# Prompt attention with scores kept keys by queries: a first pass for the maxima, division at the end

## The chip, the cores and the metric

The kernel runs on one core of one Trainium2 chip. The metric is the time of one execution on the device in microseconds (us). TensorE is called PE in the profile (PEld is its weight load), VectorE DVE, ScalarE ACT, GpSimd POOL, SyncE SP.

## The reference

A two-layer encoder for 1024 prompt tokens and 32 sample tokens, width 1024. In each layer an input projection feeds three groups of attention heads, whose outputs are normalised, projected and followed by a convolutional feed-forward block. What changes is the attention of the prompt in two groups: the forget-gate heads (FoX, six of 64 columns) and the latent heads (MLA, four with 96 columns of keys and 64 of values).

```python
s = jnp.einsum('bqhd,bkhd->bhqk', qb, k) * scale
if fk is not None:                     # FoX only: running sums of log forget gates
    s = s + F_query - F_key
s = jnp.where(allowed, s, NEG_INF)     # FoX: key <= query; MLA: by chunks of 64
p = jax.nn.softmax(s, axis=-1)
return jnp.einsum('bhqk,bkhd->bqhd', p, v)
```

## The kernel before

Stages follow one another in blocks with semaphores of their own. `mixers` (L2417) calls for each layer: FoX prompt attention, FoX sample attention, windowed (SWA) prompt and sample attention, preparation of MLA, MLA prompt and sample attention, and a norm. The three prompt stages are one function, `attend_prompt` (L921).

Heads go in pairs (three for FoX, two for MLA), and a pair in eight rounds of 128 queries. A round turns the pair's queries and keys with transposes on PE (L1040, L1041, 128 x 64 or 128 x 96), ACT copies their high part as float32r and DVE subtracts to get the low part (L1115, L1116, L1161, L1164). Scores are queries x keys: stationary queries of 128, moving keys of up to 512, three products (high x high, high x low, low x high, L1068), and on the diagonal an identity matmul that adds the mask (L1072). DVE takes the row maxima, negated (L1186); ACT takes the exponential with that as its bias and its sum beside it (L1144); DVE takes the reciprocal of the sum (L1192), and DVE or POOL multiplies the probabilities by it (L1198, L1029). PE turns each 128 x 128 of them (L1092), ACT and DVE copy them to SBUF (L1131, L1207, L1209), and PE multiplies them with the values, both heads of the pair into the two halves of one bank (L1105, 64 stationary columns, float32, so two records for a matmul in the trace). ACT copies the result to yT (L1152).

The order is written by hand: each engine walks a list of units (a round of both heads up to four key tiles, then one head a unit), turns tiles three rounds ahead, and PE does the scores of unit m, the transposes of unit m-2 and the values of unit m-3. The rows of the forget gates, high and low part, come by DMA into the operand of the keys (L1011). POOL and DVE clear what the operands pad (L1022, L1168).

Of the kernel before, what the change touches and what calls it, by code (L numbers as in the profile page):

```python
# [203 lines left out]
class Load:  # L204
# [67 lines left out]
    def scalar_first(self, act):  # L272
        k = self.k
        act.wait_ge(self.const_in, 16)
        act.activation(k.identr[:, :], k.const[:, C_ID:C_ID + P], ACT.Copy)
        act.activation(k.mfoxr[:, :], k.const[:, C_MFOX:C_MFOX + P], ACT.Copy)
        act.activation(k.mmlar[:, :], k.const[:, C_MMLA:C_MMLA + P], ACT.Copy)
        act.wait_ge(self.vec_turned, 1)
        for l in range(DEPTH):
            last = act.activation(k.vec[l][:, :], self.bank[:, 7, 2 * l * P:2 * l * P + V_N], ACT.Copy)  # L280
        last.then_inc(self.vec_ready, 1)
# [593 lines left out]
def fox_rows(nc, k, prep, frow):  # L875

    with ExitStack() as s:  # L880
        ps = s.enter_context(nc.psum_tensor("fps" + k.tag, [P, 2, 512], F32))
        psF = s.enter_context(nc.psum_tensor("fpsF" + k.tag, [P, QT, P], F32))
        sem = k.sems["fox"]
        f_done, copied, f_turned, row_hi = (sem[n] for n in ("f", "fc", "ft", "rh"))
        tri, ones = k.const[:, C_TRI:C_TRI + P], k.const[:, C_ONE:C_ONE + P]
        lf, cl, pre, fp, fs = prep.g[:, 5], prep.cl, prep.pre, prep.fp, prep.fs
        with nc.Block() as block:

            @block.sync
            def _(sp):  # L890
                sp.wait_ge(prep.stored, 16 * prep.STORES)

            @block.tensor
            def _(pe):
                pe.matmul(ps[:, 0, 0:QT * FOXH], tri, lf[:, 0:QT, :], start=True, stop=False)
                pe.matmul(ps[:, 0, 0:QT * FOXH], ones, pre[:, 0, 0:QT, :], start=False, stop=True)
                pe.matmul(ps[:, 1, 0:TT * FOXH], tri, cl[:, :, :], start=True, stop=False)
                pe.matmul(ps[:, 1, 0:TT * FOXH], ones, pre[:, 1], start=False, stop=True).then_inc(f_done, 1)
                pe.wait_ge(copied, 1)
                for t in range(QT):  # L900
                    last = pe.transpose(psF[0:FOXH, t, :], fp[:, t, :], k.const[:, C_ID:C_ID + P])
                last.then_inc(f_turned, 1)

            @block.scalar
            def _(act):
                act.wait_ge(f_turned, 1)
                act.activation(frow[0][:, :], psF[0:FOXH, :, :].rearrange("p t n -> p (t n)"), ACT.Copy,
                               scale=-1.0).then_inc(row_hi, 1)

            @block.vector  # L910
            def _(dve):
                dve.wait_ge(f_done, 1)
                dve.tensor_copy(fp[:, :, :], ps[:, 0, 0:QT * FOXH].rearrange("p (t h) -> p t h", h=FOXH))\
                   .then_inc(copied, 1)
                dve.tensor_copy(fs[:, :, :], ps[:, 1, 0:TT * FOXH].rearrange("p (t h) -> p t h", h=FOXH))
                dve.wait_ge(row_hi, 1)
                dve.scalar_tensor_tensor(frow[1][:, :], psF[0:FOXH, :, :].rearrange("p t n -> p (t n)"), -1.0,
                                         frow[0][:, :].bitcast(F32), ALU.mult, ALU.subtract)


def attend_prompt(nc, k, kind, heads, kdim, q_of, k_of, v_of, kv_of, yT, yc, frow=None, alibi=None):  # L921
# [739 lines left out]
class ProjectOut:  # L1661
# [18 lines left out]
    def cols(self, o):  # L1680
        return slice((o % NT) * TN, (o % NT + 1) * TN)
# [678 lines left out]
@contextmanager  # L2360
def own_semaphores(nc, name, singles, several=()):

    with ExitStack() as s:
        one = lambda n: s.enter_context(nc.semaphore(f"{name}_{n}"))
        sem = {n: one(n) for n in singles.split()}
        for n, m in several:
            sem[n] = [one(f"{n}{i}") for i in range(m)]
        yield sem
        restart(nc, [x for v in sem.values() for x in (v if isinstance(v, list) else [v])])
# [47 lines left out]
def mixers(nc, k, lay, places, proj, prep, used):  # L2417
# [11 lines left out]
    with ExitStack() as f:  # L2429
        keep(f, "small_kept", places.LOW - places.SMALL)  # L2430
        fs = prep.fs
        with ExitStack() as f2:
            frow = [f2.enter_context(nc.sbuf_tensor("frow" + n + k.tag, [FOXH, SEQ], F32R)) for n in ("hi", "lo")]
            fox_rows(nc, k, prep, frow)
            cols = lambda o: (lambda h: proj[:, :, o + HD * h:o + HD * (h + 1)])
            attend_prompt(nc, k, "fox", FOXH, HD, cols(O_FQ), cols(O_FK),
                          lambda h, t: proj[:, t, O_FV + HD * h:O_FV + HD * (h + 1)], lambda h: h, yT, 0, frow=frow)
        kc = f.enter_context(nc.sbuf_tensor("fkc" + k.tag, [P, QT, FOXH * HD], F32))
        vc = f.enter_context(nc.sbuf_tensor("fvc" + k.tag, [P, QT, FOXH * HD], F32))
        loads = [(dst[:, a:b, :], src[lay, 0].rearrange("(t p) h d -> p t (h d)", p=P)[:, a:b])  # L2440
                 for dst, src, a, b in ((kc, k.cache_fox_k, 0, 4), (kc, k.cache_fox_k, 4, QT), (vc, k.cache_fox_v, 0, QT))]
        tiles = [(P, lambda u, t=t: kc[:, t, P * u:P * (u + 1)], lambda p, t=t: vc[:, t, P * p:P * (p + 1)])
                 for t in range(QT)]
        tiles.append((DEC, lambda u: proj[0:DEC, QT, O_FK + P * u:O_FK + P * (u + 1)],
                      lambda p: proj[0:DEC, QT, O_FV + P * p:O_FV + P * (p + 1)]))
        attend_sample(nc, k, "fox", FOXH, lambda u: proj[0:DEC, QT, O_FQ + P * u:O_FQ + P * (u + 1)], FOXH // 2, P,
                      lambda h: HD * (h % 2), tiles, loads, yT, 0, fs, SwaHeads(nc, k, lay, f, proj))
# [15 lines left out]
    with ExitStack() as f:  # L2463
        qm = rt("qm", [P, TT, MLAH, MQK], where=f)
        km = rt("km", [P, 2 * QT + 1, MLAH, MQK], where=f)
        vm = rt("vm", [P, 2 * QT + 1, MLAH, HD], where=f)
        mla_prepare(nc, k, lay, proj, qm, km, vm)
        left.close()
        attend_prompt(nc, k, "mla", MLAH, MQK, lambda h: qm[:, :, h, :], lambda h: km[:, :, h, :],
                      lambda h, t: vm[:, t, h, :], lambda h: h, yT, 6)  # L2470
        tiles = [(P if j < QT else DEC, lambda u, j=j: km[0:P if j < QT else DEC, QT + j, u, :],
                  lambda p, j=j: vm[0:P if j < QT else DEC, QT + j, 2 * p:2 * p + 2, :].rearrange("p h d -> p (h d)"))
                 for j in range(TT)]
        attend_sample(nc, k, "mla", MLAH, lambda h: qm[0:DEC, QT, h, :], MLAH, MQK, lambda h: HD * (h % 2), tiles,
                      [], yT, 6)
# [52 lines left out]
```

## Time and profile before

| | us |
|---|---|
| median of 3 runs | 3335.85 |
| lowest and highest | 3334.83, 3339.76 |
| the profiled execution | 3335.93 |
| its span | 3333.8 |
| busy PE, DVE, ACT, POOL | 2998.4, 1566.6, 991.1, 863.2 |
| granted clock of TensorE, mean | 0.934 |

A name in a group is a tile with its stage (psSfox are the scores of the FoX stage). Shapes are partitions x elements. Matmuls are pipelined: the duration of one contains its modelled end, so their price is read from the distances between starts. "Idle before" is the time in which the engine had nothing, with what ended it.

### The profile page before, as it was taken

To read this page: it belongs to the slowest core of one execution; us is meant where nothing else is said; L and a number is where in the kernel's file an instruction comes from. 1 tells how busy PE (TensorE), PEld (TensorE's weight loads), DVE (VectorE), ACT (ScalarE), POOL (GpSimd) and SP (SyncE) were. 2 spreads that over 40 slices of the span, in tenths; PEclk is the share of its full clock that TensorE was granted. 3 is DMA by queue.
4 is the path that set the end of the run, shared out by engine and by line. 5 is a ranking of instruction groups with operands and counts; after the bars stand their busy time and mean duration, and the time that the engine had idled before them with its cause. 6 is when DMAs were issued, how large, how long until landed. Compare 5 with 4: busy or idle time off the path is not lost. (4 is left out here: it accounts for less than half of the span.)

```text
span 3333.8 us, 50479 instructions
## 1 busy us (share of the span) xinstructions
PE 2998.4 (90%) x19996; PEld 2804.0 (84%) x19996; DVE 1566.6 (47%) x2734; ACT 991.1 (30%) x2175; POOL 863.2 (26%) x489
## 2 busy tenths in 40 slices
PE   5998977686999999999999988876679999999998
PEld 5997745465999999999899975645579999999998
DVE  3326646743244444444442465657343444444443
ACT  3224525544321111111242254454333111111111
POOL 3111142103332322222341122311044222222230
PEclk8998958787999999999999988787889999999999
DMA  5110010001511111111122101000024111111111
GB/s 174 44 41 23 2 48 18 1 1 56 177 51 51 38 50 50 38 50 38 55 89 59 40 3 40 10 17 1 14 92 153 45 44 50 38 50 38 50 50 53
DMA packets 181249, 161.81 MB, mean 49 GB/s; under 512 B 17236, under 2 KB 168316, under 8 KB 180860
## 3 DMA queue, kind: packets, MB, share of 16 engines
q1 hardware_dynamic: 181116, 160.02, 15.4%
q8 instruction: 85, 1.39, 0.2%
q14 instruction: 48, 0.39, 0.0%
HBM read 129.97 MB, written 30.13 MB: 48 GB/s over the span
## 5 line engine op out<-in xcount | busy, mean ns | idle before, releaser
L1942 PE MATMUL bank_b<-x_hi,fwhi 128*128 128x352 f32 x2112 | 690.5, 327 | 5.3 <-POOL fwlo L1898 5.3
L1942 PE MATMUL bank_b<-x_hi,fwlo 128*128 128x352 f32 x2112 | 688.9, 326 | 0.0
L1942 PE MATMUL bank_b<-x_lo,fwhi 128*128 128x352 f32 x2112 | 687.3, 325 | 0.0
L1898 POOL TENSOR_TENSOR fwlo<-raw,fwhi 128x1024 fp32r<-128x1024 f32 x132 | 322.2, 2441 | 583.5 <-ACT fwhi L2023 569.8
L1942 PEld LDWEIGHTS bank_b<-x_hi,fwhi 128*128 128x128 f32 x2112 | 400.0, 189 | 6.5 <-POOL fwlo L1898 5.9
L1942 PEld LDWEIGHTS bank_b<-x_lo,fwhi 128*128 128x128 f32 x2112 | 402.2, 190 | 0.0
L1942 PEld LDWEIGHTS bank_b<-x_hi,fwlo 128*128 128x128 f32 x2112 | 398.6, 189 | 0.6
L2131 DVE TENSOR_TENSOR fx<-fx,bank_b 128x352 f32<-128x352 f32 x528 | 275.6, 522 | 233.3 <-PE bank_b L1972 233.3
L1972 PE MATMUL bank_b<-fuhi,fwhi 128*128 128x352 f32 x1056 | 344.5, 326 | 10.3 <-DVE fx L2131 5.7
L1972 PE MATMUL bank_b<-fulo,fwhi 128*128 128x352 f32 x1056 | 344.8, 326 | 0.0
L1972 PE MATMUL bank_b<-fuhi,fwlo 128*128 128x352 f32 x1056 | 344.2, 326 | 0.0
L2043 ACT ACTIVATE fuhi<-fcb 128x1024 fp32r<-128x1024 f32 x44 | 46.7, 1061 | 696.3 <-PE bank_b L1972 550.7
L1907 POOL TENSOR_TENSOR fcb<-fcb,rsb 128x1024 f32<-128x1024 f32 x44 | 96.8, 2201 | 510.9 <-ACT fcb L2037 510.9
L1972 PEld LDWEIGHTS bank_b<-fuhi,fwhi 128*128 128x128 f32 x1056 | 201.5, 191 | 14.1 <-DVE fx L2131 9.1
L543 PE MATMUL bank_a<-whi,x_hi 128*128 128x246 f32 (+1 forms) x648 | 183.4, 283 | 17.7 <-POOL x_lo L320 10.9
L1972 PEld LDWEIGHTS bank_b<-fulo,fwhi 128*128 128x128 f32 x1056 | 199.1, 189 | 0.0
L1972 PEld LDWEIGHTS bank_b<-fuhi,fwlo 128*128 128x128 f32 x1056 | 198.8, 188 | 0.0
L543 PE MATMUL bank_a<-whi,x_lo 128*128 128x246 f32 (+1 forms) x648 | 183.1, 283 | 0.0
L543 PE MATMUL bank_a<-wlo,x_hi 128*128 128x246 f32 (+1 forms) x648 | 183.1, 283 | 0.0
L543 PE MATMUL bank_b<-whi,x_lo 128*128 128x246 f32 (+1 forms) x648 | 180.8, 279 | 0.0
L543 PE MATMUL bank_b<-wlo,x_hi 128*128 128x246 f32 (+1 forms) x648 | 180.7, 279 | 0.0
L543 PE MATMUL bank_b<-whi,x_hi 128*128 128x246 f32 (+1 forms) x648 | 179.8, 278 | 0.0
(409 smaller groups left out, 5968.4 us busy)
## 6 DMA issues: line engine op xcount, KB each, us to landing
raw<-in_w_ffn_up SPq DMA_DIRECT2D x88, 512.0 KB, 3.8
raw<-in_w_ffn_down SPq DMA_DIRECT2D x44, 512.0 KB, 3.6
wraw<-in_w_in SPq DMA_DIRECT2D x18, 984.0 KB, 5.5
xs<-x_between SPq DMA_DIRECT2D x16, 528.0 KB, 3.9
x_between<-xs SPq DMA_DIRECT2D x16, 528.0 KB, 2.6
fx<-x_between SPq DMA_DIRECT2D x2, 4224.0 KB, 13.2
raw<-in_w_out SPq DMA_DIRECT2D x16, 512.0 KB, 5.2
x_between<-fx SPq DMA_DIRECT2D x3, 1408.0 KB, 6.3
```

The costliest lines, as they stand in the source:

```text
L543: last = pe.matmul(bank[0:n, t % NB, 0:WN], a[:, c, at], w[b][:, c, :], start=(c == 0 and m == 0), stop=(c == DC - 1 and m == 2))
L1898: pool.tensor_tensor(self.wlo[:, r], self.raw[:, o % 2], self.whi[:, r].bitcast(F32), ALU.subtract)\
L1907: pool.tensor_tensor(v, v, self.rsb[:, 0:SEQ], ALU.mult)
L1942: last = pe.matmul(bank[:, first_bank + t, 0:TN], w[:, role, c, :], x[:, c, self.cols(t)], start=(c == 0 and m == 0), stop=(c == DC - 1 an ...
L1972: last = pe.matmul(bank[:, 6 + o % 2, 0:TN], w[:, D0 + e, m, :], x[:, e, self.cols(t)], start=(e == 0 and i == 0), stop=(e == 1 and i == 2))
L2043: act.activation(uhi[:, e, 0:SEQ], cb[:, e, 0:SEQ], ACT.Copy)
L2131: dve.tensor_tensor(x, x, bank[:, 6 + o % 2, 0:TN], ALU.add).then_inc(self.p_out[o % 2], 1)
```

## The change

FoX and MLA prompt attention call a new function, `attend_keys`; SWA keeps `attend_prompt`. The new function goes by pair of heads and half of the queries (u, 512 queries), and in it by key tile (b, 4 or 8 of 128). Scores stand keys x queries, so that their exponentials are what the value matmul needs, without a transpose. The maximum of each query must be known before: a first pass multiplies only the high parts, queries x keys, and DVE reduces it (masked tiles by an add of a mask table and a minimum in one operation). The maxima are turned by PE, split in high and low parts and laid as extra rows into the query operand, against rows of ones in the keys, so that the score matmul subtracts them. Exponentials are summed over key tiles on POOL (first head) and DVE (second head), a matmul with ones adds them over partitions, and each half's output is multiplied by the reciprocal (512 columns, both heads) at the end. First-pass units of the next half, and the turning of later tiles, are hosted in the steps of the current one. The masks of the score matmul are made at launch, turned over. Here `bank_free(pe, item)` waits until the item two before it in the two banks psT has been read (for denominators: `inverted`).

```diff
+    XS = 2
+    NP = 3
+    nb = lambda u: HT * (u % 2 + 1)
+    first_col = lambda u, b: max(b - HT * (u % 2), 0) * P
+    def max_units(u):
+        if u % 2 == 0:
+            return [(e, j, 0, (j + 1) * P, True) for j in range(HT) for e in range(2)]
+        return [(e, j, a, w, a > 0) for j in range(HT) for a, w in ((0, HALF), (HALF, (j + 1) * P)) for e in range(2)]
+    def hosted_tiles(u, b):
+        p = u // 2
+        if u % 2 == 0:
+            return [(p, HT + 2 * b), (p, HT + 2 * b + 1)] if b < 2 else []
+        return [(p + 1, b)] if b < HT and p + 1 < pairs else []
+    def hosted_units(u, b):
...
+        if u % 2 == 0:
+            at = (0, 4, 10, 16, 16)
+        else:
+            at = (0, 0, 0, 0, 2, 4, 6, 8, 8)
+        return units[at[b]:at[b + 1]]
...
+        def sum_up(eng, u, b, e, done):
...
+                eng.tensor_tensor(acc[:, e, c:HALF], acc[:, e, c:HALF], new, ALU.add).then_inc(done, 1)
...
+            def _(pool):
+                for n, (rows, value) in enumerate(((mc[:, :, :, :, :], 1.0), (qh[R0:K2].bitcast(F32), 1.0),
+                                                   (kh[R0:K2].bitcast(F32), 1.0), (mtab[:, 0:HALF - P], 0.0))):
+                    pool.memset(rows, value).then_inc(cleared, 1)
+                    pool.wait_ge(cleared, n + 1)
...
+                def first_pass(u, units):
...
+                        if n >= 2:
+                            pe.wait_ge(maxed, n - 1)
...
+                        pe.matmul(psS[:, n % 2, 0:w], qh[0:K1, s, e, j * P:(j + 1) * P], kh[0:K1, p % 2, e, a:a + w],
+                                  start=True, stop=True).then_inc(scored, 1)
...
+                def maxima(u):
+                    pe.wait_ge(maxed, unit_base[u + 1])
...
+                            last = pe.transpose(psT[0:NA, bank_of[item] % 2, j * P:(j + 1) * P], mc[:, u % 2, j, e, :],
+                                                ident)
...
+                def scores(u, b):
...
+                        pe.matmul(out[:, c:HALF], kh[0:K2, p % 2, e, keys], qh[0:K2, s, e, c:HALF], start=True, stop=False)
+                        pe.matmul(out[:, c:HALF], kl[0:kdim, p % 2, e, keys], qh[0:kdim, s, e, c:HALF], start=False,
+                                  stop=False)
+                        last = pe.matmul(out[:, c:HALF], kh[0:K2, p % 2, e, keys], ql[0:K2, s, e, c:HALF], start=False,
+                                         stop=not diag)
...
+                def values(u, b):
+                    p, n, c = u // 2, step_no[(u, b)], first_col(u, b)
+                    pe.wait_ge(expd, 2 * n + 2)
+                    if b == 0 and u:
+                        pe.wait_ge(y_done, u)
...
+                def denominators(u):
...
+                        last = pe.matmul(psT[HD * e:HD * e + HD, bank_of[item] % 2, :], ones, acc[:, e, :],
+                                         start=True, stop=True)
...
+                pe.wait_ge(cleared, 3)
+                for i in range(HT):
+                    turn(0, i)
+                first_pass(0, max_units(0))
+                maxima(0)
+                for u, b in steps:
+                    for p, i in hosted_tiles(u, b):
+                        turn(p, i)
+                    scores(u, b)
+                    if b == 0 and u:
+                        denominators(u - 1)
+                    first_pass(u + 1, hosted_units(u, b))
+                    if b:
+                        values(u, b - 1)
+                    if b == nb(u) - 1:
+                        if u + 1 < NU:
+                            maxima(u + 1)
+                        values(u, b)
+                denominators(NU - 1)
...
+                        if diag:
...
+                            dve.tensor_tensor_reduce(ps, ps, mtab[:, HALF - w:HALF], -1.0, m if a else -BIG, ALU.add,
+                                                     ALU.min, m).then_inc(maxed, 1)
+                        else:
+                            dve.tensor_reduce(m, ps, AX, ALU.max, negate=True).then_inc(maxed, 1)
...
+                def divide(u):
+                    p, s = divmod(u, 2)
+                    dve.wait_ge(den_done, u + 1)
+                    dve.reciprocal(rec[:, :], psT[:, bank_of[("den", u)] % 2, :]).then_inc(inverted, 1)
+                    dve.wait_ge(inverted, u + 1)
+                    dve.wait_ge(mixed, step_no[(u, nb(u) - 1)] + 1)
+                    dve.tensor_tensor(yT[:, yc + p, s * HALF:(s + 1) * HALF], psO[:, :], rec[:, :], ALU.mult)\
+                       .then_inc(y_done, 1)
...
+                for u, b in steps:
+                    for p, i in hosted_tiles(u, b):
+                        low_part(p, i)
+                    if b == 0 and u:
+                        divide(u - 1)
+                    first_pass(u + 1, hosted_units(u, b))
+                    if b >= 2:
+                        sum_up(dve, u, b - 1, 1, sum1)
+                    if b == nb(u) - 1:
+                        if u + 1 < NU:
+                            maxima(u + 1)
+                        sum_up(dve, u, b, 1, sum1)
```

In `mixers` the two calls are replaced; FoX hands over tiles of 128 columns (a pair in one transpose), MLA one head at a time.

## Rows read from the trace of the kernel before

**Rows 1.** Page, part 1: busy time of each engine over the span

```profile
PE 2998.4 (90%) x19996; PEld 2804.0 (84%) x19996; DVE 1566.6 (47%) x2734; ACT 991.1 (30%) x2175; POOL 863.2 (26%) x489
```

**Rows 2.** Windows: stretch, length, busy of PE, PEld, DVE, ACT, POOL, granted clock

```profile
285.30:414.00 128.70, 117.86 (x1008) 100.99 (x1008) 86.28 (x182) 73.30 (x204) 22.31 (x17) 0.93 0.01 2
631.90:721.00 89.10, 80.73 (x672) 69.48 (x672) 55.96 (x120) 49.01 (x136) 10.02 (x8) 0.91 0.00 1
285.30:298.00 12.70, 8.05 (x35) 6.81 (x36) 6.12 (x12) 3.44 (x13) 7.89 (x6) 0.50 0.02 3
```

**Rows 3.** Timeline (start us, us, engine): first value matmuls of two head pairs

```profile
302.75 0.33 PE L1105 MATMUL psOfox<-pTfox,proj 128*64 128x128 f32 x2
340.73 0.33 PE L1105 MATMUL psOfox<-pTfox,proj 128*64 128x128 f32 x2
```

**Rows 4.** Timeline: starts of neighbouring score matmuls, 512, 384, 256 and 128 columns

```profile
1995.27 0.40 PE L1068 MATMUL psSfox<-kThifox,qTlofox 96*128 96x512 f32 x1
1995.51 0.34 PE L1068 MATMUL psSfox<-kThifox,qThifox 96*128 96x384 f32 x1
1995.68 0.34 PE L1068 MATMUL psSfox<-kTlofox,qThifox 96*128 96x384 f32 x1
...
332.20 0.28 PE L1068 MATMUL psSfox<-kTlofox,qThifox 96*128 96x256 f32 x1
332.32 0.28 PE L1068 MATMUL psSfox<-kThifox,qTlofox 96*128 96x256 f32 x1
...
2003.51 0.27 PE L1068 MATMUL psSfox<-kThifox,qTlofox 96*128 96x128 f32 x1
2003.62 0.27 PE L1072 MATMUL psSfox<-mfoxr,identr 128*128 128x128 f32 x1
```

**Rows 5.** Timeline: eight transposes; 32 records of value matmuls, what follows them

```profile
345.44 1.06 PE L1092 MATMUL psTfox<-const,prfox 128*128 128x128 f32 x8
...
336.19 1.97 PE L1105 MATMUL psOfox<-pTfox,proj 128*64 128x128 f32 x32
338.09 0.50 PE L1068 MATMUL psSfox<-kThifox,qThifox 96*128 96x512 f32 x1
338.43 0.40 PE L1068 MATMUL psSfox<-kTlofox,qThifox 96*128 96x512 f32 x1
```

**Rows 6.** Groups by form: operation, shapes, count, busy us, mean ns

```profile
L1186 DVE TENSOR_REDUCE stfox<-psSfox 128x2 f32<-128x512 f32 x3 | 2.1, 691 | 4.1 <-PE psSfox L1072 4.1
L1161 DVE TENSOR_TENSOR qTlofox<-psXfox,qThifox 64x256 fp32r<-64x256 f32 x24 | 9.8, 408 | 4.9 <-ACT kThifox L1116 4.8
L1144 ACT ACTIVATE prfox<-psSfox,stfox 128x512 f32<-128x512 f32 x6 | 4.1, 682 | 0.0
...
L1182 DVE TENSOR_TENSOR psSswa<-psSswa,biasswa 128x512 f32<-128x512 f32 x42 | 29.1, 693 | 6.3 <-PE psSswa L1068 5.4
```

**Rows 7.** Groups by form, one line (min/median/max ns): reciprocals, six-column add

```profile
L1192 DVE RECIPROCAL stfox<-stfox 128x2 f32<-128x2 f32 x12 | 1.8, 153 | 0.0
...
L665 DVE RECIPROCAL rs<-rs 128x8 f32<-128x8 f32 x1 | 0.2, 205 | 4.8 <-ACT rs L657 4.8
...
L823 DVE TENSOR_TENSOR fpre<-fpre,fcl x16: 156/158/167, 257.2 to 1897.7; 128x6 f32<-128x6 f32 x16
```

**Rows 8.** Timeline: GpSimd and VectorE, both with two SBUF inputs

```profile
998.12 2.58 POOL L1898 TENSOR_TENSOR fwlo<-raw,fwhi 128x1024 fp32r<-128x1024 f32 x1 [24.00 <-ACT fwhi L2023]
998.36 2.38 DVE L2125 TENSOR_TENSOR fulo<-fcb,fuhi 128x32 fp32r<-128x32 f32 x1
```

**Rows 9.** Timeline: a memset and the first score of the forget-gate stage

```profile
285.31 1.80 POOL L1022 MEMSET kThifox<- 32x2048 f32 x1 [50.04 <-POOLq L887]
...
292.76 0.46 PE L1068 MATMUL psSfox<-kThifox,qThifox 96*128 96x128 f32 x1
```

**Rows 10.** Timeline: last write of that stage; transposes after an idle TensorE, second layer

```profile
412.96 0.28 ACT L1152 ACTIVATE yT<-psOfox 128x128 f32<-128x128 f32 x1 [2.20 <-PE psOfox L1105]
...
2043.41 1.39 PE L1092 MATMUL psTfox<-const,prfox 128*128 128x128 f32 x8 [1.96 <-DVE pTfox L1209]
```

More of the change, by code:

```diff
@@ L275, in scalar_first @@
         act.activation(k.identr[:, :], k.const[:, C_ID:C_ID + P], ACT.Copy)
-        act.activation(k.mfoxr[:, :], k.const[:, C_MFOX:C_MFOX + P], ACT.Copy)
-        act.activation(k.mmlar[:, :], k.const[:, C_MMLA:C_MMLA + P], ACT.Copy)
+        one = k.const[:, C_ONE:C_ONE + P]
+        act.activation(k.mfoxr[:, :], k.const[:, C_TRI:C_TRI + P], ACT.Copy, scale=-BIG, bias=BIG)
+        act.activation(k.mmlar[0:CHUNK, :], one[0:CHUNK], ACT.Copy, scale=0.0)
+        act.activation(k.mmlar[CHUNK:P, 0:CHUNK], one[CHUNK:P, 0:CHUNK], ACT.Copy, scale=BIG)
+        act.activation(k.mmlar[CHUNK:P, CHUNK:P], one[CHUNK:P, CHUNK:P], ACT.Copy, scale=0.0)
         act.wait_ge(self.vec_turned, 1)
@@ L2435, in mixers @@
             cols = lambda o: (lambda h: proj[:, :, o + HD * h:o + HD * (h + 1)])
-            attend_prompt(nc, k, "fox", FOXH, HD, cols(O_FQ), cols(O_FK),
-                          lambda h, t: proj[:, t, O_FV + HD * h:O_FV + HD * (h + 1)], lambda h: h, yT, 0, frow=frow)
+            attend_keys(nc, k, "fox", FOXH, HD,
+                        lambda p, i: [(proj[:, i, o + P * p:o + P * (p + 1)], P, w, 0) for w, o in ((0, O_FQ), (1, O_FK))],
+                        lambda h, t: proj[:, t, O_FV + HD * h:O_FV + HD * (h + 1)], yT, 0,
+                        k.const[:, C_MFOX:C_MFOX + P], k.mfoxr[:, :], frow)
         kc = f.enter_context(nc.sbuf_tensor("fkc" + k.tag, [P, QT, FOXH * HD], F32))
@@ L2468, in mixers @@
         left.close()
-        attend_prompt(nc, k, "mla", MLAH, MQK, lambda h: qm[:, :, h, :], lambda h: km[:, :, h, :],
-                      lambda h, t: vm[:, t, h, :], lambda h: h, yT, 6)
+        attend_keys(nc, k, "mla", MLAH, MQK,
+                    lambda p, i: [(x[:, i, 2 * p + e, :], MQK, w, e) for w, x in ((0, qm), (1, km)) for e in range(2)],
+                    lambda h, t: vm[:, t, h, :], yT, 6, k.const[:, C_MMLA:C_MMLA + P], k.mmlar[:, :])
         tiles = [(P if j < QT else DEC, lambda u, j=j: km[0:P if j < QT else DEC, QT + j, u, :],
```

199 lines of the change are left out of this document (added).

## The prediction

> **What bounds the kernel now.** I read the page first: TensorE (PE) is busy for 90% of the span [rows 1], so the first question of every stage is how much work its PE stream holds. Then the windows of the stages that change: forget-gate (FoX) attention lasts 128.7 us in the first layer, latent (MLA) attention 89.1 us, and in both PE is busy for over 90% while VectorE (DVE) has 86 and 56 us of work [rows 2]. The second layer repeats them, so some 435 us of 3334 are at stake. Then the timeline. One pair of heads takes 340.73 - 302.75 = 38.0 us [rows 3]. Next to that I set the PE stream of one pair, by distances between starts: a score matmul costs 0.24 us at 512 columns, 0.17 at 384, 0.12 at 256, 0.11 at 128 [rows 4]. One pass over one head's causal tiles is 0.64 us for each set of 512, 384, 256, 128 and there are two such sets and four more of 512, so 2.24 us. Three passes and eight masks of 0.09 make 7.4 us a head, 14.9 a pair. A transpose costs 0.11 us (eight in 1.06, of which the last 0.27 is modelled end), so 72 of probabilities cost 7.9 and 32 of queries and keys 3.5. A 128-column value matmul is two records of 0.055 us, and 72 cost 7.9. A change to or from the 64-column value matmuls costs about 0.3 us: after 32 records the next score starts 1.90 us later instead of 1.76, and the one behind it after 0.34 instead of 0.24 [rows 5]; eight such breaks are 2.4. The sum, 36.6 us, is nearly the 38.0 measured. The stage is bound by the PE stream. Around three pairs lie a front, 7.5 us to the first score [rows 9] at half clock [rows 2], and a short tail.
>
> **PE stream after the change.** Scores are the same area turned over, again 14.9 us a pair. The first pass adds one pass for each head, +4.5. The 72 transposes go, -7.9. FoX turns two heads in one transpose, -1.8 (MLA: nothing). Value matmuls cover the same area, 7.9; they are now 12 visits instead of 8, and two for denominators come on top, so breaks go from 2.4 to 4.2. Denominators: two matmuls of 512 columns for each half, at 4 x 0.11 each, +1.8. Turning the maxima: 16 transposes, +1.8. Together 14.9+4.5+1.8+7.9+4.2+1.8+1.8 = 36.9 us against 36.6. What the transposes give, the new operations take; PE's stream gains nothing. So the answer lies in who waits.
>
> The Trainium skill, TensorEngine Tiling (Array Packing), section Key Properties, says that changing the tiling mode drains TensorE; the 0.3 us above is how this trace shows it, and by that rule each of the six extra visits a pair costs the same whatever its width.
>
> **DVE after the change.** For a pair: low parts of eight tiles, four of 128 columns each (the 256-column one takes 0.41 [rows 6]; I take 0.25 at 128), 8.0 us for FoX, 6.0 for MLA. Reductions of the first pass: eight plain ones of 512 at 0.69 [rows 6] = 5.5, and 16 masked ones. The masked one is an operation that this trace lacks. Its nearest row is the add of 512 columns into PSUM, 0.69 [rows 6]; I take that, with 0.29, 0.42, 0.56 for the shorter ones: 4 x 1.96 = 7.8. The upper bound is twice that, as if it were an add and a reduction. Running sums of the second head: 5.5. Low parts of the maxima: four of 512 columns, 2.8. Last the division, once for each half: a reciprocal of 512 columns, then a multiply of 0.69. No such reciprocal is in the trace. Eight columns take 0.205 us, two take 0.153, while a six-column add takes 0.158 [rows 7]: 0.052/6 = 8.6 ns a column, eight times an ordinary one. So 512 columns take 0.15 + 512 x 0.0083 = 4.4 us. Bounds: 0.69 (as an ordinary operation) and 4.6. I take 4.4, since the slope is read from rows of this very operation. Two divisions make 10.2 us a pair. DVE's sum is 39.8 us a pair, 120 for FoX instead of 86: more than PE's 111.
>
> The Trainium skill, VectorE: DVE Perf Modes, "First, the fixed hardware budget", says that the reciprocal is an iterated divide with a repeat count of 8. By that rule 512 columns take 8 x 512 cycles; the rows above agree in slope.
>
> **Where these waits fall.** DVE and PE run in order, and the first pass has two PSUM buffers, so PE stops at the third unit of a batch until DVE has reduced the first.
>
> Half of queries 0-511 (even), which hosts the 16 units of the next half. PE holds 14 us of work, DVE 16.4 and the division 5.1. The chain: PE turns two tiles, scores, denominators, to 3.4; division to 8.6; four reductions to 10.4; PE, stopped until then, turns two tiles, ACT and DVE split them to 14.0; six reductions to 17.9; PE values and scores to 19.2; six reductions and a sum to 24.2; the last maxima are turned, copied (0.6), split (0.7) for two heads, to 27.9. Before the next half's scores nothing can go. So 28 us, 22.5 without a division for the first.
>
> Half of queries 512-1023 (odd). PE holds 22.3 us. The second score of step 1 takes the bank of the denominators, so it waits for the reciprocal: 4.4 less 0.9 of work, 3.5 lost. The maxima at its end lose 1.3 behind the last values. So 27 us, 23 in the last pair, which hosts nothing.
>
> Front: PE first waits for three memsets on GpSimd, the largest of 4096 columns. 2048 take 1.80 us [rows 9], so 0.2+1.8+3.6 = 5.6 us in which it used to turn tiles. Four tiles through two buffers, ACT and DVE to 13.1, eight first-pass reductions to 17.0, the maxima to 20.7. FoX 20.7 instead of 7.5, MLA about 17 instead of 6.
>
> Tail: denominators, reciprocal, multiply after the last value matmul: 1.4+4.4+0.8 = 6.6.
>
> FoX: 20.7+22.5+27+28+27+28+23+6.6 = 182.8 instead of 412.96+0.28-285.3 = 127.9 [rows 10]: +55. MLA: 17+21.5+27+27+23+6.6 = 122.1 instead of 88: +34. Both layers: +178.
>
> Granted clock: PE stood for 2.0 us in the second layer and the eight transposes behind it took 1.39 instead of 1.06 [rows 10], [rows 5]; the front runs at 0.50, the 1.2 GHz level [rows 2]. The new stage lets PE stand for 3.5 to 5 us at each division. I take 1 us lost at each of the 16 inner ones, with bounds 0 and 3: +16.
>
> ACT loses the accumulator reads and the copies of turned probabilities; a 512-column exponential is 0.68 us or less [rows 6], 35 us in a FoX stage, beside 26 of splits, under PE. GpSimd sums the first head beside it. The four extra constants at launch lie under loads: 0, at most 1 us. SyncE's row transfers wait for the second memset group and land before the first unit in my front.
>
> Sum against the profiled execution (3335.9 us with what lies around the span, the median of the runs within 0.1 us): 3336+178+16 = **3530 us**.
>
> **Rivals.** (a) The reciprocal streams at one column a cycle, 0.7 us. An even half then loses 3.7 us, an odd one 3.5, the tail 3.7, and the clock stays: 20 divisions x 3.6 = 72, and 16 less, 3442 us. Against it: the slope in [rows 7]. (b) GpSimd and DVE block each other. A 32-column subtraction with two SBUF inputs took 2.38 us and ended with GpSimd's operation begun before it [rows 8]. The new running sums run on both engines with two SBUF inputs. Each DVE sum could wait up to 1 us; 9 a pair, of which a third falls where DVE is the bound: 3 x 10 pairs = +30, and with it the masked reduction at double price, +3.9 for each even half: +39. 3600 us. For it: the row; against: in the odd halves DVE has slack.
> The Trainium skill, GPSIMD Engine Reference, section Key points, says the two engines share SBUF interfaces; by this rule the wait of (b) is due on each overlapping sum, and the row on blocking agrees.
> (c) Faster: the long value matmuls hide the mode change. Then the 14 breaks cost nothing, -4.2 a pair, and if the reciprocal also costs under 1 us, DVE (30 us a pair) is hidden in PE's 32.7: FoX 98+15 (front beyond the work already counted)+3 = 116, -12; MLA -8; 3296 us. It decides from a reciprocal under 1 us and a break under 0.1. (d) The change works as meant but only balances, PE bound with reciprocal cheap and breaks as now: FoX 111+15+3 = 129, within 0.2%: 3336.
>
> **How the numbers follow.** Forecast 0.62, (a) 0.14, (b) and more lost clock 0.14, (c) 0.06, (d) 0.04. The range leaves out (c), (d) and the outer part of (b): 3420 (rival (a) less 20 for my waits being too long) to 3600. Faster by over 0.2% (what a measurement of this kernel can tell) 0.06, within 0.2% 0.04, slower 0.90.
>
> **What would show it.** The reciprocal's row near 4.4 us, twenty of them; PE idle released by it for about 3.5 us in odd halves; first-pass matmuls waiting for DVE's reductions in even ones; the first full score some 20 us into the stage; the FoX window near 185 us and MLA near 125. A reciprocal row of 0.7 us, or DVE sums of 1 us and more, would prove the term wrong.

## The result: 389 us slower, twice the forecast

| | before | after |
|---|---|---|
| median, us | 3337.4 | 3726.2 |
| lowest and highest | 3334.8, 3339.8 | 3695.1, 3739.1 |
| span of the profiled execution | 3333.8 | 3731.8 |
| granted clock of TensorE, mean | 0.934 | 0.863 |

The ratio is 1.1155, with a 95% interval of 1.1122 to 1.1187. The forecast was 3530 us, its range ended at 3600: the direction was right, the time outside. +389 us came where +194 were forecast.

The profile page of the kernel after, part 1, stands against [rows 1]; its two lines for PE and the clock in 40 slices follow.

```profile
PE 3300.8 (88%) x18700; PEld 2812.8 (75%) x18700; DVE 1669.5 (45%) x2976; ACT 959.9 (26%) x2033; POOL 919.9 (25%) x569
...
PE   6997996757599999999999899885767999999999
...
PEclk9995556867799999999999855577768999999999
```

PE counts 302 us more of busy time with fewer instructions, while its stream was forecast to be no longer. The clock line says where: in slices 4 to 6 and 24 to 26, the FoX stages, TensorE was granted half its speed. The windows of the kernel after (stretch, length, busy of PE, PEld, DVE, ACT, POOL, granted clock) answer to [rows 2]: the FoX stage, three of its halves of queries (an odd one, queries 512 to 1023; an even one, 0 to 511; the last, odd as well, which hosts no first pass), the MLA stage.

```profile
281.00:562.60 281.60, 244.00 (x601) 112.82 (x600) 116.91 (x274) 69.53 (x181) 35.47 (x38) 0.54 0.00 1
345.50:395.50 50.00, 47.08 (x117) 21.23 (x117) 18.46 (x47) 13.18 (x33) 7.28 (x7) 0.57 0.00 1
395.50:431.70 36.20, 31.80 (x83) 15.59 (x83) 19.82 (x44) 9.64 (x27) 2.56 (x5) 0.55 0.00 1
520.10:561.90 41.80, 38.35 (x83) 15.64 (x83) 8.09 (x9) 6.48 (x13) 6.74 (x7) 0.53 0.00 0
783.60:916.40 132.80, 105.08 (x432) 60.91 (x432) 72.62 (x150) 38.18 (x88) 24.16 (x25) 0.78 0.00 1
```

DVE has 117 us of work in 282: it isn't the bound it was forecast to be. PE is busy 244 us at a clock of 0.54, where the stage before had 0.93.

So I went to the spacing of the score matmuls, the view of [rows 4]. Timeline of the kernel after, PE and its weight loads (start, duration, line, in brackets the idle time before): a FoX score at full clock, then one at half clock.

```profile
337.96 0.50 PE L1119 MATMUL psTfox<-qhifox,khifox 67*128 67x512 f32 x1 [0.38 <-DVE qlofox L1227]
338.39 0.18 PEld L1120 LDWEIGHTS psTfox<-qhifox,klofox 64*128 64x128 f32 x1 [0.24 <-issue]
338.39 0.50 PE L1120 MATMUL psTfox<-qhifox,klofox 64*128 64x512 f32 x1
338.82 0.19 PEld L1122 LDWEIGHTS psTfox<-qlofox,khifox 67*128 67x128 f32 x1 [0.25 <-issue]
...
342.35 0.78 PE L1119 MATMUL psTfox<-qhifox,khifox 67*128 67x512 f32 x1
343.06 0.79 PE L1120 MATMUL psTfox<-qhifox,klofox 64*128 64x512 f32 x1
343.78 0.79 PE L1122 MATMUL psTfox<-qlofox,khifox 67*128 67x512 f32 x1
```

Matmuls of 512 columns start 0.43 us apart at full clock, against 0.24 in [rows 4], and 0.71 us apart at half. The weight load waits for "issue", no engine. The operands tell why: 67, then 64, then 67 contraction rows. A head's 64 columns, two rows for the forget gate and one for the maximum make 67; the low part of the keys has no such rows, and the code takes `kl[0:kdim]`, 64. The kernel before padded all to 96. MLA has 97, 96 and 97 rows, and its spacing is not widened (0.24 us at full clock). So the theory A of the experiments: a product of 64 rows between products of 67 drains TensorE twice (I call a drain the gap that such a change leaves), and a drained TensorE is then kept slow.

To see where each run's time lies I give the stages from the timelines: FoX from the first gate matmul to the end of the last write of yT (the gate work before the stage, about 5 us, is in all of them), MLA from the last write of the windowed heads to its own last one. Each of the other stretches agrees within 5 us in all runs.

| run | median, us | FoX, layers 1 and 2 | MLA, layers 1 and 2 |
|---|---|---|---|
| before | 3337 | 132.9, 132.9 | 172.4, 172.8 |
| after | 3726 | 284.8, 279.9 | 219.7, 222.8 |
| e1_pad | 3629 | 221.8, 222.8 | 221.2, 220.3 |
| e2_copy | 3642 | 253.3, 248.6 | 206.3, 206.1 |
| e3_before64 | 3398 | 163.6, 163.5 | 173.1, 172.4 |
| e4_pad_copy | 3541 | 184.4, 203.9 | 206.1, 205.2 |
| e5_three | 3573 | 216.1, 217.5 | 205.5, 205.4 |
| e6_nofirst | 3477 | 190.1, 172.3 | 187.3, 188.2 |
| e7_all | 3588 | 215.5, 224.9 | 207.4, 210.0 |
| e9_nofirst_raw | 3507 | 230.6, 225.7 | 172.8, 175.4 |
| e10_fill | 3566 | 203.7, 215.7 | 207.1, 203.6 |
| e11_fill_raw | 3729 | 296.3, 300.0 | 204.1, 209.4 |
| e12_before_fill | 3331 | 130.9, 130.0 | 171.0, 170.6 |

After against before: +152 and +147 in FoX (forecast 55 and the clock), +47 and +50 in MLA (forecast 34 and the clock).

### The profile page after: what moved, and what is told of

Its sections match the earlier page's. It is cut to its first block and busy times, and to the rows that moved or that the text cites. A ratio compares the mean times of both kernels' runs of the same rounds, so it can differ in the third digit from the quotient of the medians.

```text
span 3731.8 us, 48237 instructions
## 1 busy us (share of the span) xinstructions
PE 3300.8 (88%) x18700; PEld 2812.8 (75%) x18700; DVE 1669.5 (45%) x2976; ACT 959.9 (26%) x2033; POOL 919.9 (25%) x569
```

## Experiments: the drains, the divisions, and both

**e1_pad**

```diff
+                pool.memset(kl[R0:K2].bitcast(F32), 0.0).then_inc(cleared, 1)
...
-                        pe.matmul(out[:, c:HALF], kl[0:kdim, p % 2, e, keys], qh[0:kdim, s, e, c:HALF], start=False,
+                        pe.matmul(out[:, c:HALF], kl[0:K2, p % 2, e, keys], qh[0:K2, s, e, c:HALF], start=False,
```

> The change with the three rows 64 to 66 of the low keys cleared and the second FoX score product made with 67 contraction rows instead of 64, so that all products of a FoX score have the same rows; the output stays the same. Theory A (a product of 64 rows between products of 67 drains TensorE twice, and the drained engine is then held at the 1.2 GHz level): the 512-column spacing in a FoX score goes from 0.43 us (full clock) and 0.71 us (half clock) to 0.24 and 0.43, the granted clock of the FoX stage rises from 0.50-0.59 to the 0.8 of MLA, the FoX stage goes from some 281 us to about 190, near the 183 of the prediction, and the time falls by about 170 us to some 3555. Rival B (the clock is low because TensorE stands at divisions and behind the reductions of the first pass; the drains are only their own 0.2 to 0.3 us): 72 scores a stage, two changes each, give 30 us a stage, the clock stays under 0.6, and the time is about 3665. Rival C (contraction rows don't matter): 3726.

Measured 3629.2 us (3612.7 to 3634.1), ratio to before 1.0883 (1.0864 to 1.0902): -97 us by the medians, all of it in FoX (-63 and -57 in the profiled executions, of which that of e1_pad was its fastest). That lies between A (3555) and B (3665), nearer to B. The windows of the padded run: an odd, an even and the last half of FoX.

```profile
338.10:370.10 32.00, 28.77 (x117) 15.36 (x117) 19.58 (x48) 12.96 (x33) 6.23 (x7) 0.77 0.01 1
370.10:402.00 31.90, 25.98 (x83) 14.70 (x83) 19.84 (x46) 9.50 (x27) 3.63 (x5) 0.60 0.00 1
464.20:498.60 34.40, 30.91 (x83) 15.71 (x83) 8.12 (x10) 6.48 (x13) 6.15 (x7) 0.55 0.00 0
```

The odd half fell from 50.0 to 32.0 us, its clock rose from 0.57 to 0.77. The even half hardly moved and stayed at 0.60. So the drains are one cause, and there is a second that lowers the clock.

**e2_copy** and **e4_pad_copy**

```diff
-                    dve.reciprocal(rec[:, :], psT[:, bank_of[("den", u)] % 2, :]).then_inc(inverted, 1)
+                    dve.tensor_copy(rec[:, :], psT[:, bank_of[("den", u)] % 2, :]).then_inc(inverted, 1)
```

> The change with a plain copy of 512 columns in the place of each of the 20 reciprocals; it leaves out the division, so its output is not the reference's. Theory A (the low clock comes from the drains): each division gives back up to 3.36 - 0.69 = 2.7 us, 53 us in all if every one lies on the path, fewer in the FoX stages, whose clock stays under 0.6: 3675 to 3700. Rival B (TensorE standing at the divisions keeps the clock down): the clock of FoX returns to over 0.8 and the time falls by 150 us or more, to below 3580.

> Both edits at once: rows padded to 67 and a copy instead of the reciprocal (leaves out the division, so its output is not the reference's). It shows what the change costs beside these two. Theory A: some 3555 less 53 to 70 us (each division 2.7, or more where the clock is lost behind it): 3490 to 3500, the FoX clock over 0.85, and what is left over the 3336 of the kernel before lies in the fronts (13 us each) and in the halves bound by VectorE. Rival B: the same time as with the copy alone, less 60.

Measured 3642.4 us (3612.0 to 3655.0; 1.0901, 1.084 to 1.0962) and 3540.8 (3528.2 to 3543.8; 1.0616, 1.0598 to 1.0634). Both lie between the theories, 3675 for A and 3580 for B in the first, 3500 and 3582 in the second. Without the reciprocal 84 us go from the drained kernel and 88 from the padded one: 4.2 and 4.4 us a division, where 3.36 - 0.69 = 2.7 is all that DVE saves. The rest I put down to the clock, and the windows say how. First e2_copy: two odd halves of FoX in one execution, 120 and 119 matmuls, and the last half. Then e4_pad_copy: an odd half, and the last half in the first and in the second layer.

```profile
343.10:394.20 51.10, 51.10 (x120) 22.78 (x119) 15.89 (x48) 14.75 (x38) 7.41 (x7) 0.50 0.00 1
426.70:456.50 29.80, 29.09 (x119) 13.84 (x118) 16.64 (x48) 14.41 (x37) 7.29 (x7) 1.00 0.00 1
490.30:530.50 40.20, 39.47 (x86) 16.11 (x85) 5.50 (x10) 7.08 (x14) 7.22 (x7) 0.50 0.00 0
```

```profile
393.00:417.10 24.10, 23.05 (x119) 13.17 (x117) 16.77 (x48) 13.96 (x37) 7.43 (x7) 1.00 0.00 1
446.20:464.10 17.90, 17.11 (x84) 9.05 (x83) 8.00 (x10) 7.08 (x14) 7.26 (x7) 1.00 0.00 0
2180.60:2212.90 32.30, 31.52 (x85) 15.97 (x84) 5.44 (x10) 7.08 (x14) 7.24 (x7) 0.50 0.00 1
```

The same work took 29.8 or 51.1 us, and 17.9 or 32.3 us, by the level of the clock with which it was entered, and kept that level from its start to its end. The second pair has no change of rows: a padded stream too can stay at half clock for a whole half, with PE busy for 31.5 of 32.3 us.

The two kernels differ in the rows alone, so halves at one level of the clock price a change of rows: 29.8 - 24.1 = 5.7 us for the 32 changes of an odd half at full clock, 0.18 us each, and 40.2 - 32.3 = 7.9 us for the 32 of the last half at half clock, 0.25 us each. For the 288 changes of both layers that makes 51 and 71 us, an estimate from these halves. So more than half of the 97 us of e1_pad is the changes' own price; the rest I put down to the clock, which rose in the odd halves.

The two levels are also the likeliest reason for the spread of the kernel after (44 us where the kernel before has 5); that I have only argued.

**e3_before64**

```diff
+                                    rows = slice(0, HD if fox and x else None)
-                                    last = pe.matmul(bank[:, 0:n], qT[x][:, r % RQ, e, :],
-                                                     kT[y][:, p % 2, e, f + a:f + a + n],
+                                    last = pe.matmul(bank[:, 0:n], qT[x][rows, r % RQ, e, :],
+                                                     kT[y][rows, p % 2, e, f + a:f + a + n],
```

> The kernel before, with the last of its three FoX score products made with 64 contraction rows instead of 96 (the 32 rows left out are zeros, the output stays the same). It adds only the change of rows, twice in each of the 72 scores of a stage, to a stage without division at the end and without a first pass. Theory A: each change costs 0.2 us, 29 us a stage at full clock, and the granted clock of the stage falls from 0.93 as well; together between 3395 (clock kept) and 3520 (clock at half), I expect 3480. Rival B: 3395 and the clock above 0.85. Rival C: 3336.

Measured 3397.8 us (3395.2 to 3399.3), ratio 1.0186 (1.0169 to 1.0203): +60.5 us, rival B's number to 3 us. The mean granted clock of the span is 0.930 (before 0.934). The windows of this run say what part is clock: the beginning of the FoX stage, and 40 us in its middle.

```profile
299.00:313.80 14.80, 14.80 (x54) 9.45 (x53) 6.26 (x15) 6.07 (x19) 4.40 (x3) 0.50 0.01 1
...
340.00:380.00 40.00, 39.91 (x291) 27.96 (x291) 24.01 (x55) 21.88 (x62) 5.01 (x4) 1.00 0.01 1
```

At full clock a pair of heads takes 398.06 - 352.33 = 45.7 us between its last writes of yT, where the kernel before has 376.19 - 338.21 = 38.0: 7.75 us for 24 scores with two changes each, 0.16 us a change, 46 us in six pairs. The other 14 us are the clock: it came back at 313.8 us, in the kernel before at 299.9, though PE did not stand in between. Once back it stayed for 119 us. The Trainium skill, TensorEngine Tiling (Array Packing), sections Tiling Modes and Key Properties, has a mode for up to 64 contraction rows beside that for 128 and says that a change of mode drains TensorE; this run agrees.

## Experiments: what lowers the clock

**e6_nofirst** and **e9_nofirst_raw**

```diff
     def hosted_units(u, b):
-        if u + 1 == NU:
-            return []
+        return []
```

> The change with padded rows, and without the first pass of all halves but the first: its matmuls and reductions are left out, with the exponential taken at a scale of 0.001 so that it stays finite (its output is not the reference's). The divisions, the turning of the maxima and all else stay. Theory D: the clock of the even halves goes from 0.5-0.6 to above 0.9, an even half from 32-34 us to about 17 (11 of TensorE's work, 3.5 at the division, 3 at the maxima) and an odd one from 28-32 to 25 to 28: about 3440. Rival E (the stand of 3 to 4 us at each division lowers the clock by itself): the even halves lose only the 6 us of work and stops of the first pass, the clock stays under 0.7: about 3570.

> The change with 64 rows left as they are (not padded), without the first pass of all halves but the first, and with a copy instead of the reciprocal (leaves out both, exponentials at a scale of 0.001; its output is not the reference's). The drains stay, and hardly any stop is left. Theory F (drains don't lower the clock, they only keep a lowered one from coming back): the FoX clock is above 0.9, odd halves take 29 to 30 us, even ones about 17, and the time is about 3440. Rival A (the drains alone pull the clock down): the FoX clock stays under 0.65, odd halves take 50 us, and the time is about 3590.

Measured 3476.6 us (3459.7 to 3500.2; 1.0437, 1.0382 to 1.0493) and 3507.1 (3482.1 to 3527.7; 1.0489, 1.0435 to 1.0544), in the middle of the rivals both (3440 and 3570, 3440 and 3590). The diff shows the edit that they share; e6 has the padded rows beside it, e9 the copy. Without the first pass the padded kernel gives back 153 us. MLA's even half fell from 31.5 to 14.2 us at a clock of 1.00 (theory D; 18.2 at 0.72 in the second layer), a part of it the work left out, but the FoX halves behind a division are still slow, at 0.50 to 0.72, and the last one has its 34.4 us again (theory E). Both kinds of stop lower the clock: DVE's hold on the first pass and the division.

Behind its front e9 has neither, and drains alone. The windows of e9_nofirst_raw: an odd half of FoX, the last half of FoX, and an odd half of MLA.

```profile
402.80:451.30 48.50, 48.50 (x115) 21.03 (x114) 12.36 (x31) 14.93 (x39) 7.60 (x7) 0.50 0.00 1
468.50:508.70 40.20, 39.40 (x85) 16.03 (x85) 5.45 (x10) 7.10 (x14) 7.22 (x7) 0.50 0.00 0
764.00:787.20 23.20, 23.03 (x127) 13.61 (x125) 11.94 (x23) 12.59 (x29) 8.13 (x7) 1.00 0.00 1
```

Here PE is counted busy for all 48.5 us and stays at the 1.2 GHz level: I had expected 30 us and 1.00 (theory F). And the drained stream did not only fail to come back, it also fell. Three windows of its second layer, one behind the other:

```profile
2131.00:2179.10 48.10, 48.10 (x110) 20.20 (x110) 11.21 (x27) 13.76 (x34) 7.42 (x7) 0.50 0.00 1
2179.30:2189.40 10.10, 10.10 (x44) 5.31 (x44) 7.50 (x21) 6.24 (x19) 1.98 (x3) 1.00 0.00 0
2189.60:2240.60 51.00, 50.23 (x115) 20.52 (x115) 7.09 (x12) 10.03 (x20) 7.68 (x8) 0.50 0.00 0
```

From 2131.0 to 2189.4 us PE is counted busy without a break, and yet the clock rose and fell again. So the fall needs no stop. MLA, without drains, runs at 1.00 and takes 172.8 us, as the kernel before (172.4): there, the first pass and the division were the whole price of the change.

**e10_fill** and **e11_fill_raw**

```diff
+                def fill(u, count):
+                    p, s = divmod(u, 2)
+                    for _ in range(count):
+                        pe.matmul(psD[:, :], kh[0:K2, p % 2, 0, 0:P], qh[0:K2, s, 0, :], start=True, stop=True)
...
+                        if b is not None and u % 2:
+                            fill(u - 1, {(0, 2): 12 if u > 1 else 3, (1, 2): 5, (2, 2): 2, (2, 4): 1}.get((b, z), 0))
...
+                        if u % 2 and b == 1 and e == 1:
+                            fill(u, 10)
```

> The change with padded rows (3629 us) and useless matmuls of 512 columns into the free eighth PSUM bank, put where TensorE stands: 10 after the first score of step 1 in each odd half, where it waits for the reciprocal (2.4 us), and in the even halves 12 before the third unit of the first pass in step 0 (3 in the first half), 5, 2 and 1 before later units that wait for VectorE. Some 120 fillers a FoX stage and 75 an MLA stage, 0.24 us each at full clock: 94 us of added work in all. The output is unchanged, and nothing is taken away. Theory G (the price of a stop is the low clock behind it, not the stop): the clock of the attention stages goes from 0.5-0.77 to over 0.9 and the kernel gets faster by its added work: even halves from 32-34 to about 26, the last one from 34.4 to about 22; 3629 falls to about 3540. Rival H (the stops cost what they last, the clock low for another reason, such as VectorE's pace): 3629 to 3660.

> The same fillers in the change as it is, rows of 64 left (3726 us), output unchanged. It asks whether a TensorE that never stands keeps its clock in spite of the drains. Theory G and F (drains don't lower the clock, they keep a lowered one from coming back): FoX odd halves fall from 50 to about 33, the FoX clock rises over 0.85, the time is that of the padded and filled kernel plus 60: about 3600. Rival A (drains alone hold it down once the clock was low in the front, and it never gets back to full): FoX halves stay at 50 and 36 us, only MLA gains: 3700 to 3726.

The fillers were fewer than I wrote: 162 in the FoX stages and 102 in the MLA stages by the trace, 264 x 0.24 = 63 us at full clock. e10: 3565.7 us (3556.1 to 3579.5), ratio 1.0697 (1.0677 to 1.0716), 64 us faster than the padded kernel that does 63 us less, and nearer to theory G's 3540 than to H's 3629. The windows of e10_fill: an odd half, the last half of FoX, an even half of MLA.

```profile
343.00:369.80 26.80, 25.84 (x129) 15.45 (x129) 19.38 (x47) 12.80 (x33) 6.22 (x7) 1.00 0.01 2
462.00:482.50 20.50, 17.06 (x83) 9.05 (x83) 10.25 (x9) 6.49 (x13) 5.99 (x6) 0.99 0.00 1
778.90:803.50 24.60, 20.45 (x101) 12.79 (x101) 17.35 (x37) 6.24 (x15) 3.74 (x5) 1.00 0.00 1
```

The last half, still with its reciprocal, took 20.5 us instead of 34.4; MLA's even half 24.6 instead of 31.5. Nothing was taken away, only TensorE was kept at work. That shows theory G for these halves: most of a stop's price is the slow clock behind it. The even halves of FoX stayed at 0.54 to 0.63 and took 32 to 34 us, fillers or not.

In the drained kernel the same fillers brought nothing in FoX: 3729.0 us (3701.1 to 3738.9), ratio 1.1144 (1.1108 to 1.118), 3 us above rival A's range and far from theory G's 3600. MLA gained 16 and 13 us, FoX lost 12 and 20. The window from 320 to 396.5 us of e11_fill_raw, and then the list of PE's waits in it (sum, times, longest):

```profile
320.00:396.50 76.50, 75.88 (x188) 36.68 (x186) 26.48 (x65) 16.38 (x41) 8.61 (x9) 0.50 0.00 1
```

```profile
PE psSfox L1101 <- issue: 0.5, 1, 0.5
```

For 76.5 us PE stood once, for 0.5 us, and the clock did not come back. Between e10 and e11 only the rows differ: in e10 the clock first came back 56 and 72 us after the first gate matmul of the two layers, here 117 and 116. With e3 this shows that changes of rows make the clock come back later, and e10, e12 and e5 show that filled or shorter stops bring it back. Neither is the whole rule. A drained stream ran a whole half at full clock (e2), another fell without a stop (e9), and a padded one stayed at half clock without a stop (e4). What sets the level in a stream that doesn't stand, and why, no run tells.

The Trainium skill, TensorE: Matmul & The Clock Gate, Part 1, ties the slow clock to an idle array and the full one to sustained activity. For the stops these runs agree. For the window above and the 32.3 us of e4_pad_copy, busy in the profile and slow, they don't; the measurement decides.

## Experiments: mending it

**e5_three** and **e7_all**

```diff
-                        if n >= 2:
-                            pe.wait_ge(maxed, n - 1)
+                        if n >= 3:
+                            pe.wait_ge(maxed, n - 2)
```

and, in e7_all alone,

```diff
-                pe.wait_ge(cleared, 3)
                 for i in range(HT):
                     turn(0, i)
+                pe.wait_ge(cleared, 3)
...
+                    act.activation(den[:, :], psT[:, bank_of[("den", u)] % 2, :], ACT.Copy).then_inc(copied, 1)
...
-                    dve.reciprocal(rec[:, :], psT[:, bank_of[("den", u)] % 2, :])
+                    dve.reciprocal(rec[:, :], den[:, :])
```

> The change with padded rows (3629 us) and a third PSUM bank for the scores of the first pass (the stage uses seven of eight), so that TensorE runs three units ahead of VectorE's reductions instead of two. In the padded run the clock falls from 1.00 to 0.5-0.6 at the first such stop of each half of queries 0-511 and stays there for about 20 us. Theory D (these short stops start the low clock): the stops at the steps without a division go, the even halves that had 32 to 34 us come to 24 to 28, 10 such halves in all, and the time falls by 40 to 80 us to 3550 to 3590. Rival E (the division starts it: VectorE is held 4 us, three units pass instead of two, TensorE still stands some 3 us): the clock of the even halves stays under 0.7 and the time is 3610 to 3629.

> A mended change, output unchanged: padded rows; three PSUM banks for the first pass; TensorE waits for the cleared rows only after it has turned the first four tiles; ScalarE copies the denominators from PSUM to SBUF and VectorE takes the reciprocal from there, so that the second score of the next step gets its bank after a copy of 0.6 us instead of a reciprocal of 3.36 us. Against the padded run (3629): the front gives 8 us in a FoX stage and 3 to 4 in an MLA stage, 23 in all; each of the 10 odd halves loses its stop of 2.4 us, 24 in all; what the clock returns comes on top. Theory D: 3629 - 23 - 24 - 60 (as with three banks) = 3520. Rival E: 3580. In neither does it come near 3337, since TensorE's sum of a pair is no smaller than before.

A third bank gave 57 us: 3572.6 (3567.4 to 3576.5), ratio 1.0705 (1.0688 to 1.0723), as theory D had it for the time. MLA's even half fell from 31.5 to 24.7 us and its clock rose from 0.66 to 0.88; FoX's, forecast at 24 to 28, went from 31.9 to 29.3 only, its clock from 0.60 to 0.62.

The further edits of e7_all (front, copy of the denominators) made it 15 us slower than that: 3587.7 (3577.6 to 3597.3), ratio 1.0758 (1.073 to 1.0786). I had expected 3520, or 3580 by theory E, which held three banks to be of no use; with the 57 us that they gave, neither theory has this. The front did get shorter: the first full score starts 300.74 - 277.80 = 22.9 us after the first gate matmul instead of 303.88 - 278.66 = 25.2, 2.3 us of the 4.8 by which the turning starts earlier, because TensorE now waits 4.3 us for the forget gates' row by DMA. The stop at the division only moved: PE's longest wait for DVE between 366 and 430 us is now this one, of the value matmuls for the output bank.

```profile
PE psOfox L1139 <- DVE yT L1250: 3.2, 1, 3.2
```

And MLA's even half is back at 0.57 and 32.1 us. In this run the shorter queue for the bank was worth nothing, since the reciprocal still stood before the next use of the output bank.

**e12_before_fill**, the kernel before:

```diff
                 for r in range(AHEAD):
                     turn_tile(r)
+                    for _ in range({"fox": (13, 6, 0), "mla": (6, 6, 0), "swa": (0, 0, 0)}[kind][r]):
+                        pe.transpose(psS[:, 0, 0, 0:P], ident, ident)
```

> The kernel before, with useless transposes between the first three turns of tiles in the FoX stages (13 and 6) and the MLA stages (6 and 6), where TensorE waits for VectorE's low parts (3.09 and 1.51 us in FoX, 1.5 and 1.5 in MLA); output unchanged. Its clock is 0.50 in the first 14 us of a FoX stage and comes back at 299.9, 7 us after the work became continuous. Theory G: with continuous work from 285.3 on it comes back 5 to 7 us earlier, which gives 2 to 3 us a stage in four stages: 3326 to 3330, a version faster than both. Rival H: 3336 to 3340.

Measured 3331.1 us (3326.7 to 3333.2, 11 runs) beside 3337.05 (15 runs): ratio 0.998, interval 0.9971 to 0.9989, 1 us above theory G's range. This version is faster than both. In the timeline of e12_before_fill the wait of 3.09 us for DVE's low parts is filled, and a transpose costs 0.11 us from 290.87 on; in the kernel before the clock came back at 299.9.

```profile
284.75 2.98 PE L1047 MATMUL psSfox<-const 128*128 128x128 f32 x13
288.04 0.42 PE L1040 MATMUL psXfox<-const,proj 128*64 128x128 f32 x1 [0.31 <-DVE kTlofox L1166]
...
290.87 0.27 PE L1040 MATMUL psXfox<-const,proj 128*64 128x128 f32 x1
```

The stages gained 2.0 and 2.9 us (FoX), 1.4 and 2.2 (MLA).

## Why the prediction failed, step by step

- **"Scores are the same area turned over, again 14.9 us a pair."** The failed step. It counted columns and left out that FoX's three products have 67, 64 and 67 rows. I had taken 0.3 us for each change around the value matmuls, and cited the rule, but did not go through the new matmuls for others. Each score has two changes, 144 scores in both layers. The sum had nothing for them. Their own price is 46 to 51 us at full clock (e3, e2 against e4) and 71 at half clock; the time fell by 97 when they were taken away (e1).
- **"I take 1 us lost at each of the 16 inner ones, with bounds 0 and 3: +16."** Too small, and in the wrong places. A lowered clock costs 51.1 - 29.8 = 21 us in a drained half (e2) and 34.4 - 20.5 = 14 us in the last half of the padded kernel (e1 against e10), since it stays low for a whole half. And the stops of the first pass, for which I took none, lower it too: a third bank, which shortens them alone, brought 57 us, and fillers at both kinds of stop 64 while adding 63. The row behind the price, eight transposes in 1.39 us instead of 1.06 after a stop [rows 5, 10], is where a single stop stands; I carried it to halves that have several.
- **Reciprocal 4.4 us.** It took 3.36 us, twenty times. The slope of [rows 7] was right in kind (6.3 ns a column between 2 and 512, not 8.3), and the bound of 0.69 far off; the eight cycles a column that I had worked out beside it are too many by the same measure. The stop behind it in an odd half was 2.4 us at most (e1) against the 3.5 forecast. One stage of it, by form of the kernel after:

```profile
L1233 DVE RECIPROCAL recfox<-psTfox 128x512 f32<-128x512 f32 x6 | 20.1, 3357 | 15.1 <-PE psTfox L1143 15.1
L1227 DVE TENSOR_TENSOR qlofox<-psTfox,qhifox 3x512 fp32r<-3x512 f32 x12 | 8.2, 682 | 26.8 <-ACT qhifox L1178 26.8
L1041 DVE TENSOR_TENSOR accfox<-accfox,pTfox 128x512 f32<-128x512 f32 x9 | 6.2, 688 | 16.1 <-ACT pTfox L1194 16.1
L1218 DVE CUSTOM_DVE_ANT_0 psSfox<-psSfox,mtabfox,mcfox 128x512 f32<-128x512 f32 x6 | 4.3, 756 | 0.9 <-PE psSfox L1093 0.9
```

  Rival (a) put the reciprocal's whole effect at 3530 - 3442 = 88 us; e4 against e1 measured 88 (with a copy of 0.69 us in its place). The agreement is partly luck: fewer microseconds in the operation, more in the clock.
- **Other terms of DVE** held: running sums 0.69 in FoX, parts of the maxima 0.68, the masked reduction 0.76 at 512 against 0.69. DVE has 117 us in a FoX stage against 120. It is not the bound, because PE's time swelled past it.
- **Rival (b), the two engines blocking each other.** Its mechanism is real, its price was not. In FoX the running sums of DVE and GpSimd did not meet, and DVE's took 0.69 us. In MLA some did, and the same sum of 512 columns took 0.99 us on average and 1.35 at most; the group of both layers, and the sum that took longest in the first:

```profile
L1041 DVE TENSOR_TENSOR accmla<-accmla,pTmla 128x512 f32<-128x512 f32 x12 | 11.9, 994 | 18.2 <-ACT pTmla L1194 18.2
...
839.72 1.27 POOL L1041 TENSOR_TENSOR accmla<-accmla,pTmla 128x512 f32<-128x512 f32 x1 [1.31 <-ACT pTmla L1194]
840.19 1.35 DVE L1041 TENSOR_TENSOR accmla<-accmla,pTmla 128x512 f32<-128x512 f32 x1
```

  That is 12 x 0.31 = 3.7 us in all, on an engine that was not the bound, where the rival had 30.
- **Halves.** With fillers and at full clock (e10) the last half, forecast at 23 us, took 20.5, the odd half of 27 took 26.8, and the even one of MLA, 27 as well, 24.6. For these the layout of waits was right. In the kernel after the FoX halves ran slow and drained: odd 50.0, even 36.2, last 41.8. The even half of FoX, forecast at 28, ran at full clock in no run, so its layout is not shown. The tail, from the end of the value matmuls' turn at 556.55 to the last write at 562.59, is 6.0 against 6.6.
- **Front.** 20.7 us forecast for FoX. After the first gate matmul the first turn came 5.0 us later in the kernel before, so the stage begins at about 282.8 in the kernel after; the first full score starts at 305.27, 22.4 us later. The memset of 4096 columns took 3.50 us, as set, and PE stood 8.2 us at it.
- **Forecast of the whole against the parts that held.** Of the kernels that do all the work of the change the padded and filled one (3566) comes nearest to the 3530 forecast. MLA costs 35 and 31 us more than before in it, forecast 34; FoX costs 71 and 83, forecast 55. That the forecast would be right at full clock throughout is not shown.

The range ended at 3600, the time of rival (b). The clock's own upper bound, 3 us a stop, would have added only 16 x 2 = 32 us to 3530, and a change of rows was no case at all. The direction did not hang on the reciprocal: rival (a), without its 4.4 us, still had 3442. The size did hang on it in part, and there an overpriced division stood in for changes of rows and a slow clock that the sum did not have.

## What to carry to other kernels

Go through the contraction rows and output columns of every matmul of a new stage, in order, not only its area: a product of 64 rows between two of 67 costs two drains, and three cleared rows remove them. Price a stop of TensorE by the clock of what follows it: read the granted clock behind it in the trace, and try useless matmuls in the gap before shortening the wait. A kernel whose halves come in two lengths in one execution (17.9 and 32.3 us here) has a clock problem, not a work problem.

## What the hardware showed that I had not expected

- A change of contraction rows between 64 and more costs 0.16 (e3) to 0.18 us (e2 against e4) at full clock and 0.25 at half clock over whole halves. Between two starts it shows as 0.43 - 0.24 = 0.19 us at full clock and 0.71 - 0.43 = 0.28 at half, where the padded spacing is 304.90 - 304.47 = 0.43 (e5_three).
- TensorE counted busy for 75.88 of 76.5 us can stay at half clock (e11), and so can a stream without a change of rows, busy for 31.52 of 32.3 us (e4). In e2 a drained stream ran a whole half at full clock; in e9 one fell from full to half clock after 58 us without a stop.
- A running sum of DVE that begins beside one of GpSimd can take 1.35 us instead of 0.69.
- Adding 63 us of useless matmuls made a kernel 64 us faster.
